# Two layer borders worked in token halves in a two-layer encoder trunk on one NeuronCore

## The reference

```python
D_MODEL, SEQ, D_FF = 1024, 512, 2816

def rmsnorm(x, gain):
    y = x * lax.rsqrt(jnp.mean(x * x, axis=-1, keepdims=True) + EPS)
    return y * gain

def swiglu(h, w_in, w_out):
    gate, up = jnp.split(h @ w_in, 2, axis=-1)
    return (jax.nn.silu(gate) * up) @ w_out

for l in range(2):
    x = x + 0.5 * rmsnorm(swiglu(rmsnorm(x, g[0]), ffn_w_in[l, 0], ffn_w_out[l, 0]), g[1])
    m = mla(rmsnorm(x, g[2]), ...) if l == 0 else hgrn2(rmsnorm(x, g[2]), ...)
    x = x + rmsnorm(m, g[3])
    x = x + 0.5 * rmsnorm(swiglu(rmsnorm(x, g[4]), ffn_w_in[l, 1], ffn_w_out[l, 1]), g[5])
```

## Time and profile before

| | |
|---|---|
| three runs | 2020.52, 2020.62, 2021.34 us |
| profiled execution | 2020.65 us, its span 2018.8 us |
| granted TensorE clock | 1.00 |
| TensorE busy | 2009.8 us of the span |
| VectorE, ScalarE, POOL busy | 935.9, 717.5, 683.9 us |
| HBM read | 176 MB, 88 GB/s over the span |

### The profile page before, as it was taken

One profiled execution on the slowest core, in us unless ns is written; L12 is line 12 of the kernel. 1 busy time (PEld: TensorE's weight loads), 2 busy tenths in 40 slices (PEclk: granted clock), 3 DMA queues, 4 the chain that ended last, 5 costly groups with the idle time before them and its releaser, 6 DMA issues.

```text
span 2018.8 us, 28331 instructions
## 1 busy us (share of the span) xinstructions
PE 2009.8 (100%) x11138; PEld 1668.2 (83%) x11138; DVE 935.9 (46%) x1229; ACT 717.5 (36%) x977; POOL 683.9 (34%) x316
## 2 busy tenths in 40 slices
PE   9999999999999999999999999999999999999999
PEld 7888888889888888888888888888888888888887
DVE  6433421588384333016534311476787766333212
ACT  5222232455342222224222222365756542222221
POOL 4444444230224444442444444200000014444444
PEclk9999999999999999999999999999999999999999
DMA  4233234200222233333232333222222123323332
GB/s 167 94 99 98 91 97 127 103 22 1 73 84 94 94 98 97 97 94 105 82 95 94 95 96 96 89 85 84 70 68 64 64 74 100 98 94 95 95 97 89
DMA packets 54516, 179.49 MB, mean 89 GB/s; under 512 B 6048, under 2 KB 10400, under 8 KB 54432
## 3 DMA queue, kind: packets, MB, share of 16 engines
q1 hardware_dynamic: 54000, 176.73, 27.7%
q10 hardware_dynamic: 432, 1.57, 0.2%
HBM read 176.18 MB, written 2.10 MB: 88 GB/s over the span
## 4 chain that ended last, share of the span: by engine, by line
PE 97%; DVE 2%; ACT 1%; issue 0%; DVEq 0%
PE psum L676 28%; PE psum L678 27%; PE psum L677 27%; PE psum L832 2%; PE psum L1096 1%; PE psum L833 1%; PE psum L838 1%; PE psum L1085 1%; PE psum L1203 1%; PE psum L1073 0%; PE psum L858 0%; PE psum L1070 0%; PE psum L1076 0%; PE psum L1074 0%; PE psum L864 0%
## 5 line engine op out<-in xcount | busy, mean ns | idle before, releaser
L591 POOL TENSOR_TENSOR w_lo<-raw,w_hi 128x1024 fp32r<-128x1024 f32 (+1 forms) x276 | 648.0, 2350 | 1113.4 <-ACT w_hi L1519 1113.4
L676 PE MATMUL psum<-xg_hi,w_hi 128*128 128x512 f32 x1734 | 681.9, 393 | 0.9 <-DVE xg_lo L2416 0.8
L678 PE MATMUL psum<-xg_hi,w_lo 128*128 128x512 f32 x1734 | 675.4, 389 | 0.0
L677 PE MATMUL psum<-xg_lo,w_hi 128*128 128x512 f32 x1734 | 675.1, 389 | 0.0
L1519 ACT ACTIVATE w_hi<-raw 128x1024 fp32r<-128x1024 f32 (+1 forms) x332 | 343.1, 1037 | 838.8 <-DMA raw<-w_up 463.9
L676 PEld LDWEIGHTS psum<-xg_hi,w_hi 128*128 128x128 f32 x1734 | 325.5, 188 | 69.6 <-issue 1.2
L678 PEld LDWEIGHTS psum<-xg_hi,w_lo 128*128 128x128 f32 x1734 | 325.5, 188 | 68.3
L677 PEld LDWEIGHTS psum<-xg_lo,w_hi 128*128 128x128 f32 x1734 | 325.7, 188 | 67.3 <-issue 1.2
L676 PE MATMUL psum<-hid_hi,w_hi 128*128 128x512 f32 (+1 forms) x726 | 278.1, 383 | 0.0
L677 PE MATMUL psum<-hid_lo,w_hi 128*128 128x512 f32 (+1 forms) x726 | 277.8, 383 | 0.0
L678 PE MATMUL psum<-hid_hi,w_lo 128*128 128x512 f32 (+1 forms) x726 | 277.8, 383 | 0.0
(11 more groups left out here) (280 smaller groups left out, 1668.0 us busy)
## 6 DMA issues: line engine op xcount, KB each, us to landing
raw<-w_up SPq DMA_DIRECT2D x172, 512.0 KB, 3.5
raw<-w_down SPq DMA_DIRECT2D x64, 512.0 KB, 3.5
raw<-w_hgrn SPq DMA_DIRECT2D x48, 512.0 KB, 3.5
raw<-w_down SPq DMA_DIRECT2D x32, 384.0 KB, 3.1
raw<-w_mla SPq DMA_DIRECT2D x16, 512.0 KB, 3.6
raw<-w_up SPq DMA_DIRECT2D x16, 128.0 KB, 4.1
xt<-x_t SPq DMA_DIRECT2D x8, 256.0 KB, 4.2
out<-xt SPq DMA_DIRECT2D x16, 128.0 KB, 1.7
```

Source lines behind the costliest of these rows:

```text
L591: pool.tensor_tensor(w_lo[slot][:, 0:n], raw[slot][:, 0:n], w_hi[slot][:, 0:n].bitcast(F32), ALU.subtract).then_inc(w_ready, 1)
L676: first = pe.matmul(ps, w_hi[slot][:, at:at + n], hi, start=start, stop=False)
L677: pe.matmul(ps, w_hi[slot][:, at:at + n], lo, start=False, stop=False)
L678: return first, pe.matmul(ps, w_lo[slot][:, at:at + n], hi, start=False, stop=stop)
```

## The change

`HALVED` names the sublayers whose entry is done in halves: the fourth (feed-forward after feed-forward) and the fifth (HGRN2 after feed-forward). For these two borders:

- TensorE's last down group becomes `split_group`: side 0 (tokens 0 to 255) over all 22 blocks, into one bank, then side 1 into another. Side 0's statistics are at block 4 of side 1 (`SPLIT_ROOT`), its spread at block 7 (`SPLIT_WIDE`). The three tiles are released only from side 1's passage over them, and the last by side 1's statistics.
- `post_statistics`, `widen` and both `keep_clock` are not run there.
- TensorE's entry becomes `entry_halves`: the same four groups, each product in two halves of 256 tokens, in an order written out by hand, with side 1's statistics and spread inside.
- ScalarE and VectorE get their own `enter_halves`: the chain square, root, reciprocal, norm, residual, high part, low part on 256 tokens at a time, 16 half chunks, side 0 first, side 1's square, copy, root and reciprocal in between.
- ScalarE splits tiles 2 and 3 of the next sublayer inside this chain, behind half chunks 1 and 3 of side 0, tile 4 behind half chunk 6; tiles 5 and 6 behind half chunks 4 and 6 of side 1. VectorE's part of tile 4 is behind half chunk 7.
- Counts of the semaphores follow (`HEADS_AFTER`, `add_squares(2)`, `out_of_psum`). SP's and POOL's code is the same.

The diff, cut to its core:

```diff
+HALVED = tuple(s for s in range(1, len(SUBLAYERS)) if SUBLAYERS[s - 1][0] == "ffn" and SUBLAYERS[s][0] != "mla")
+HEADS_AFTER = (4 + len(HALVED)) * KB + 3
+SPLIT_ROOT, SPLIT_WIDE = 4, 7
...
-                    final_group()
+                    if s + 1 in HALVED:
+                        split_group()
+                    else:
+                        final_group()
...
+            def split_group():
+                blocks_of = [(part, b) for part, blocks in enumerate(DOWN_PARTS) for b in range(blocks)]
+                tiles = []
+                for side, at in enumerate(SIDES):
+                    ps = open_group(LONG_RING)
+                    for f, (part, b) in enumerate(blocks_of):
+                        if side == 0 and b == 0:
+                            tiles.append(open_tile())
+                        if side == 1 and f == SPLIT_ROOT:
+                            pe.wait_ge(sq_ready, squared.next(KB))
+                            side_statistics(0, True).then_inc(stat_done, 1)
+                        if side == 1 and f == SPLIT_WIDE:
+                            side_widened(0)
+                        first, last = mm3(ps[:, at], (tiles[part], b * P, P), hid_hi[:, f, at], hid_lo[:, f, at],
+                                          f == 0, f == FB - 1)
+                        if side == 0 and f == 0:
+                            tile_before_is_free(first)
+                        if side == 1 and b == 0 and part:
+                            first.then_inc(w_free, 1)
+                    last.then_inc(group_done, 1)
+                    if side == 0:
+                        pe.wait_ge(sq_added, added.next(KB - 1))
+                        side_statistics(0, False)
...
+            def entry_halves():
...
+                side_statistics(1, False, close)
+                opened(0)
+                tile_before_is_free(half(0, 0, 0)[0])
+                for c in (1, 2):
+                    half(0, 0, c)
+                pe.wait_ge(sq_ready, squared.next())
+                side_statistics(1, True).then_inc(stat_done, 1)
+                for c in (3, 4):
+                    half(0, 0, c)
+                opened(1)
+                for c in range(5):
+                    half(1, 0, c)
+                side_widened(1)
+                for c in (5, 6):
+                    for g in range(2):
+                        half(g, 0, c)
+                opened(2)
+                for c in range(7):
+                    half(2, 0, c)
+                for g in range(3):
+                    half(g, 0, KB - 1)
+                opened(3)
+                for c in range(KB):
+                    half(3, 0, c)
+                for c in range(KB - 2):
+                    for g in range(ENTRY):
+                        half(g, 1, c)
+                for g in range(ENTRY):
+                    half(g, 1, KB - 2)
+                    first, last = half(g, 1, KB - 1)
...
-                if s:
+                if s and s not in HALVED:
                     post_statistics()
```

ScalarE's list:

```diff
+            def enter_halves(s, pre):
...
+                side_squared(0)
+                side_root(0)
+                half(0, 0)
+                half(0, 1)
+                hi_part()
+                half(0, 2)
+                side_squared(1)
+                half(0, 3)
+                hi_part()
+                half(0, 4)
+                side_root(1)
+                half(0, 5)
+                half(0, 6)
+                hi_part()
+                half(0, 7)
+                for j in range(KB):
+                    half(1, j)
+                    if j in (4, 6):
+                        hi_part()
```

VectorE's list:

```diff
+            def enter_halves(s, pre):
...
+                copied(0)
+                reciprocals(TB // 2)
+                order = [(side, j) for side in range(2) for j in range(KB)]
+                half_normed(0, 0)
+                half_residual(0, 0)
+                for i, (side, j) in enumerate(order):
+                    if i + 1 < len(order):
+                        half_normed(*order[i + 1])
+                    half_low(side, j)
+                    if (side, j) == (0, 3):
+                        copied(1)
+                    if (side, j) == (0, 5):
+                        reciprocals(TB // 2, TB // 2)
+                    if i + 1 < len(order):
+                        half_residual(*order[i + 1])
+                    if (side, j) == (0, 7):
+                        split(s, ENTRY - 1)
```

More of the change, by code:

```diff
@@ L905, in ffn @@
             def ffn(s):
-                entry((0, 0, 0, 2) if s else None)
+                entry("halves" if s in HALVED else (0, 0, 0, 2) if s else None)
                 for g in range(ENTRY + 1, ENTRY + EXTRA):
@@ new lines, in entry_halves, with opened, half @@
+            def entry_halves():
+                evicted_before = bank_free.count
+                tiles, banks = [], []
+                arrived = [0]
+                def opened(g):
+                    tiles.append(open_tile(by_dve=g == ENTRY - 1))
+                    if FINAL_GROUP_BANKS[1] == ENTRY_BANKS[g]:
+                        pe.wait_ge(drained, evicted_before)
+                    banks.append(open_entry_group(g))
+                def half(g, side, c):
+                    if arrived[0] == side * KB + c:
+                        pe.wait_ge(chunk_ready, chunk.next())
+                        arrived[0] += 1
+                    at = SIDES[side]
+                    return mm3(banks[g][:, at], (tiles[g], c * P, P), xg_hi[:, c, at], xg_lo[:, c, at], c == 0, c == KB - 1)
+                chunk_h.more += 2 * KB
+                side_statistics(1, False, close)
[28 more added lines that the diff above has]
+                    first, last = half(g, 1, KB - 1)
+                    if g:
+                        first.then_inc(w_free, 1)
+                    last.then_inc(group_done, 1)
@@ L943, in side_statistics @@
+            def side_statistics(side, last_chunk, at_first=None):
                 at = SIDES[side].start
@@ L948, in side_statistics @@
                                      skip_group_check=True)
+                    if at_first and b == 0:
+                        at_first(last)
                 return last
@@ L1599, in enter_chunks, with side_squared, side_root, half @@
                     hi_part()
+            def enter_halves(s, pre):
+                end = groups_to_end[0]
+                groups_to_end[0] += 1 + GROUPS_OF[SUBLAYERS[s][0]]
+                ends[0] = last_bank[s]
+                wide.more += 2
+                def side_squared(side):
+                    at = SIDES[side]
+                    act.wait_ge(group_done, end + side)
+                    act.activation(sq[:, (KB - 1) % 2, at], psum[:, FINAL_GROUP_BANKS[side], at],
+                                   ACT.Square).then_inc(sq_ready, 1)
+                def side_root(side):
+                    act.wait_ge(stat_done, stat.next())
+                    n = side * (TB // 2)
+                    act.activation(root[:, n:n + TB // 2], sums_of(FINAL_STAT[side], 0, TB // 2), ACT.Sqrt,
+                                   bias=eps[:, :], scale=1.0 / D_MODEL).then_inc(root_done, 1)
+                def half(side, j):
+                    at = SIDES[side]
+                    act.wait_ge(chunk_new, new.next())
+                    act.activation(xg_hi[:, j, at], xt[:, j, at], ACT.Copy, scale=gain(pre, j)).then_inc(chunk_hi, 1)
+                    act.activation(y[:, j, at], xt[:, j, at], ACT.Square).then_inc(pre_sq, 1)
+                act.wait_ge(sq_added, added.next())
+                added.more += 1
+                side_squared(0)
[17 more added lines that the diff above has]
+                        hi_part()
             def enter_end():
@@ L1637, in ffn @@
                 for j in range(KB):
+                    if s + 1 in HALVED and j == KB - 1:
+                        out_of_psum.more += 2
+                        break
                     if not (final and j == KB - 1):
```

57 lines of the change are left out of this document (43 added, 14 removed).

## The result

| | before | after |
|---|---|---|
| median (lowest to highest), five runs each | 2021.22 (2020.52 to 2021.52) us | 2031.34 (2030.55 to 2032.18) us |
| ratio, with its 95% interval | | 1.0051 (1.0036 to 1.0065) |
| profiled execution, its span | 2020.65, 2018.8 us | 2030.55, 2028.7 us |
| granted TensorE clock | 1.00 | 0.997 |
| border 1, border 2 (start of the last down group to the end of the entry) | 42.97, 42.97 us | 48.02, 48.27 us |

The changed kernel is slower by 10.1 us, 0.5%. In the two profiled executions the span grew by 9.9 us and the two borders by 5.05 + 5.30 = 10.35 us, so within 0.5 us nothing is gained or lost elsewhere.

A forecast was written before the change was run, and what follows sets the result against it. TensorE, busy in all of the span, bounds the kernel. Split products, added statistics and waits for chunks end a border at 46.85 us against 42.97, 3.9 slower, 7.8 for two: 2028.4 us from 2020.62, range 2020.5 to 2033.

The forecast's parts named there:

- main case: Both borders: chain waits and POOL's holds make the kernel slower, 2028.4 us, within 2025.5 to 2030.5; chance 0.55.
- the case of no difference: Whole kernel: POOL's holds miss the chain, a border ends at 43.4, total 2021.4 us; chance 0.15.
- The price of halves: Last group and entry: 162 split products at 0.0133 us each cost 2.2 us per border.
- The chain: Beside side 1: VectorE starts norming at 11.70, then each of 16 half chunks takes 1.52 us.
- The tiles: ScalarE splits tile 2 at 15.74, POOL follows at 16.87; low part 2 ends at 19.62, low part 4 at 24.75.
- TensorE's waits: In the entry, TensorE waits 1.69, 0.64 and 3.17 us for chunks 2, 3 and 4; chunk 4 at 24.80.
- Behind chunk 4: Rest of the entry: 60 group-chunks at 0.36, spread 0.22, restarts 0.23; end at 46.85, no further waits.
- Rival (3): TensorE's clock falls in the borders' idle time, each losing 1.9 us more; 2032.2 us, chance 0.22.
- The sign that the text named for it: Behind the waits, half products over 0.15 us apart would show a fallen clock and the main case wrong.
- Rival (1): POOL's holds don't reach VectorE's chain; chunk 4 at 21.3, border ends at 43.4, 2021.4 us; chance 0.15.
- Rival (2): The chain keeps ahead of TensorE, low part 4 ready by 18.8; 2.0 us less per border, 2016.6; chance 0.05.
- its best: A border where nothing waits: 324 x 0.120 + 2.1 = 41.0 us, 2.0 less than now.

The follow-up runs named there:

- e4: Kernel before, order and chain untouched, with all products of the last down group and entry at both borders issued as two of 256 columns; 2024.98 us, ratio 1.0018.
- e5: Changed kernel with POOL's subtractions for tiles 2 and 3 on 8 columns, their low parts left out, three stand-in calls ahead of chunk 4; 2020.82 us, ratio 1.0000.
- e2: Changed kernel with stand-in products in TensorE's waits at both borders: 2, 1 and 6 calls ahead of half chunks 2, 3 and 4; 2028.67 us, ratio 1.0036.
- e8: e7 with tile 2's high-part products for half chunks 0 to 4 issued early inside the waits, and fewer stand-ins; 2024.24 us, ratio 1.0018.
- e1: Changed kernel with POOL's subtractions for tiles 2 and 3 on 8 columns, third products reading the high part, low parts left out; 2022.3 us, ratio 1.0005.
- e7: Changed kernel with POOL's subtractions in 8 pieces of 128 columns, stand-ins 2 and 4 calls ahead of half chunks 3 and 4; 2026.35 us, ratio 1.0026.

## Why the prediction was right, and what it mis-sized

Predicted were 2028.4 us, in 2020.5 to 2033, and slower; measured were 2031.34. The direction, the mechanism and its place were right; the number was 2.9 us short, and 0.8 above the upper bound of the main case (2025.5 to 2030.5), because one term was put at nothing in the sum and left to a rival. The wide range took that in; it also held the case of no difference. Step by step, all at border 1 and counted from the group's start:

- **The price of halves** stood: 0.12 a half product in the changed kernel, and 1.87 us a border in e4 for the 2.2 of the sum. The shortfall of 0.3 lies in the entry (10 ns a split there, 13 in the group). The entry before had 0.64 us of waits, in which longer products would lie for nothing; that this is the reason was not tested.
- **The chain.** Norming starts at 11.73 (predicted 11.70), low parts follow one another at 921.27 and 922.80, 1.53 apart (1.52), high part 0.51 (0.50 between bounds of 0.38 and 0.72).
- **The tiles.** ScalarE splits tile 2 at 15.67 (15.74), POOL begins at 16.81 (16.87). Low part 2 takes 2.23 us (17.29 to 19.62, 2.33, predicted); low part 4 ends at 24.34 (24.75). The prediction lets each end 0.36 after POOL and doesn't show where this comes from; 0.28 and 0.27 were measured.
- **TensorE's waits**: 1.25, 0.51 and 2.71, in sum 4.5, for 1.69, 0.64 and 3.17, in sum 5.5. The prediction counted from start to start, the idle list from a product's end, which explains some 0.16 of each; of the rest, 0.4 is that chunk 4 came at 24.40 and not at 24.80. A sum made of rows of unlike places (half width from the kernel's end, full width from the borders) held to 0.4 us in 25.
- **Behind chunk 4** the sum had 22.05 us to the entry's end, which would be 46.45; measured is 48.02. The 1.57 more are the clock: 18 products at 0.213. Rival (3) had priced it at 1.9 a border from the earlier trace rows, and the total it gave, 2032.2, is 0.9 from the median. The price was right in part by luck: it came from the kernel's opening, where the slow starts span 4.8 us, and here 3.9 and 4.9 us of work lay in the slow stretch. **The term that was mis-sized is the clock: nothing in the sum, with a chance of 0.22 beside it**, for lack of a row behind a gap; it measured 1.7 and 2.1 us. The sign that the text named for it (half products over 0.15 us apart behind the waits) is what the timeline shows. The Trainium skill (TensorE: Matmul & The Clock Gate, "Why this matters for your kernels") warns of the clock behind idle gaps; the trace agrees that they do it (0.50 from 929.6 on), but its gaps of 1.25 and 0.51 us are shorter than those that the section names.

Rival (1), that POOL does not reach the chain, falls with the 2.23 us of low part 2. Its price was right all the same: e5 makes its condition true and takes 2020.8 where 2021.4 was said. Rival (2), the chain ahead of TensorE, falls by 5.6 us at chunk 4 (24.40 for 18.8), and in e5 even without holds (chunk 4 at 21.24, behind three stand-in calls).

Taken apart by the runs, border 1's 5.05 us are: 0.2 that the scheme costs with neither ill (e5); 3.0 from the holds (e2 less e5, 48.92 - 45.93, all of it ahead of chunk 4: 24.23 for 21.24); 1.7 from the clock and 0.2 from a chunk 4 that came later (changed kernel less e2). Before, the border's idle time was a single wait of 5.6 us with nothing behind it but stand-ins; the change filled that, and paid 4.3 us of narrower products and added statistics for it, so that its best was 2.0. What it then moved into the chain cost more than that.

Not tried: giving tile 2 and 3 a place of their own, so that they are split ahead of the border as before, or letting VectorE make their low parts. Either would take the holds away with all work done, the second at a price in VectorE's chain (its own low part of a whole tile takes 1.23 us, at 938.19 in the changed kernel). What e5 shows without holds, no difference from the kernel before, is the nearest measurement. It is no bound for the first, since in e5 ScalarE's splits of both tiles still stand inside the chain.

## What to carry to other kernels

Before work is cut finer to hide a chain, follow what the cut holds longer: here tiles kept through two passes moved ScalarE's and POOL's splitting from an idle stretch into the very chain that was to be hidden, and half-wide VectorE instructions wait for a whole POOL instruction as full-wide ones do. Price the cut itself first from rows of the same shape (two halves 0.24 us for one whole 0.227), since it comes off a gain of only a few us. And where a change leaves TensorE short waits in place of stand-in products, put the price of a fallen clock into the sum, not beside it. Read each border by itself, too, before a gain in the total is put down to an edit: e8's 2 us came from a tile that landed earlier.

## What was not expected

- At border 1 the clock fell behind waits of 1.25 and 0.51 us, ahead of the long one, and only 18 products ran slow, from 932.4 to 936.3. In e1 a wait of 1.36 us, with one of 0.21 ahead of it, went with a fallen clock at border 1; the same wait without the short one did not at border 2 (47.36 and 45.65 us). The three groups of e1's times, with their granted clocks, suggest that the number of such borders differs from run to run of the same kernel. What decides it is open.
- The landing of the second tile leaves no reserve and varies: ScalarE waited 0.62 and 0.41 us for it in the changed kernel, 1.52 in e2 and 2.21 in e7, at the same place. The three releases of a halved group come close together, and in 924 to 932 the queues move 262 GB/s, a DMA share of 0.75, where the kernel before has 199 and 0.53 in the same stretch. That the bunching is the cause was not tried.
- Cutting POOL's instruction shortens its hold and lengthens its work: 16 pieces take 7.98 us where two whole ones take 4.71; why was not taken apart.
